# A hybrid decoder layer: prompt heads with the values stationary, two heads in the column halves of TensorE

## The chip, the core and the metric

The kernel runs on one core of one Trainium2 chip, as one launch. The metric is device time in microseconds (us). Three runs of the kernel before gave a median of 1142.3 us (1142.15 to 1143.41). PE is TensorE, ACT ScalarE, DVE VectorE, POOL GpSimd, SP SyncE.

## The reference

One layer for two request groups with the same weights: a prompt of 256 tokens, and 8 sequences that each decode one token after a paged cache of 2048. All is float32.

```
h = x + 1/2 * gate * SwiGLU(norm(x))                        first feed-forward
[q | kv | k_pe | glu | gate_logits] = norm(h) @ w_in
A = latent attention(q, kv, k_pe) @ w_attn_out
B = swish(LayerNorm(DWConv31(GLU(glu)))) @ w_conv_out
h = h + gate_m * ((sigmoid(gA) * A + sigmoid(gB) * B) @ w_out)
y = h + 1/2 * gate * SwiGLU(norm(h))                        second feed-forward
```

What the change touches is the prompt's attention, for 16 heads of 64 value columns, causal over 256 positions:

```
s = einsum('bqhd,bkhd->bhqk', qb, k) * scale
s = where(k_pos <= q_pos, s, -inf)
p = softmax(s, axis=-1)
o = einsum('bhqk,bkhd->bqhd', p, v)
```

## The kernel before

All arrays lie with 128 rows on partitions. Each engine runs one list of instructions, written out by hand, and semaphores tie the lists together (`eng.wait_ge(sem, n)` waits until `sem` has reached `n`, `.then_inc(sem, 1)` counts up at an instruction's end). Nothing reorders the lists: an instruction that waits holds up all that stand behind it on its engine. The layer goes through stages: first feed-forward, projections, **prompt heads**, **128 cache pages** (8 sequences of 16 pages), **gates** (the gate logits' products, with the sums that close both attentions between them), output projections, second feed-forward.

*Prompt heads.* Queries fall in two blocks of 128, so a head has three 128 x 128 blocks of scores: block 0 sees keys 0 to 127, block 1 sees 0 to 255. TensorE makes them in one PSUM bank (`scores`, L2285 and L2286, two banks in turn), VectorE adds the mask and writes all 384 columns to SBUF as `sS`, then takes the maxima of both blocks (`mask_max`, L1581 to L1585), ScalarE takes the exponentials with their row sums `ls` (L1010, L1011), TensorE turns the three blocks (`turn_probs`, L2306, banks 2 and 3), and ScalarE copies them to `pTs` (`turned`, L1003). Then `values` (L2318 to L2321) multiplies: the turned probabilities are the stationary side and 64 columns of `vtok` the moving one, so that queries lie on partitions. After each four heads VectorE multiplies the result with the reciprocals of `ls` into `otok` (`heads_out`, L1593, L1596), token by token. The loop runs scores two heads ahead and values one head behind.

*Around the loop.* `turn_state` (L2295) turns the convolution's state, and ScalarE copies it into `stbuf` (`state_columns`, L996): once in head 15, once after it. `turn` (L2334 to L2341) turns a cached page, ScalarE rounds it to `kTH` (`page_hi`, L1026) and VectorE makes the rest `kTL` (`page_lo`, L1609); `keys` (L1892 to L1894) then multiplies with the weights, three products for each (high and low halves). Page 0's turn stands between the last two heads. GpSimd sets buffers, makes the first convolution rows of the sample group (`sample_rows`, L647 to L655), and later squares the rotary keys of each sequence (L674), which VectorE sums (`rope_squares`, L1651) in page 14 of the sequence.

*Gates.* `turn_heads` (L2424) turns `otok` in four groups of four blocks so that heads lie on partitions, and ScalarE copies them to `oT` (`heads_turned`, L1087), then to `oH` (L1100), the high half for the output projection.

*Page values.* For a sequence's cached values TensorE is used in four column strips of 32 (`page_values`, L2365): four products with 32 stationary columns go to four different groups of 32 partitions of PSUM.

## Time and profile before

| | |
|---|---|
| median of three runs | 1142.3 us |
| the profiled execution | 1141.46 us, of which its span 1139.6 us |
| TensorE | busy 1121.9 us (98%), granted clock 0.997 of full |
| VectorE | busy 779.2 us (68%) |
| ScalarE | busy 581.6 us (51%) |
| GpSimd | busy 68.0 us (6%) |
| chain that ended last | TensorE 94%, VectorE 2% |

The span runs from the first instruction to the last on the core; the time of a run adds what lies around it. The durations of products overlap (a product starts before its predecessor's end), so that what one costs is read from start to start. "PEld" is the loading of the stationary side, which overlaps the products. An instruction on float32 data runs in two passes on TensorE (x2 in the rows), but a turn runs in one.

### The profile page before, as it was taken

What the parts mean: (1) busy time and instruction counts of PE and PEld (TensorE: products, weight loads), DVE (VectorE), ACT (ScalarE), POOL (GpSimd) and SP (SyncE); (2) the same over time, 40 slices, a digit from 0 to 9 for tenths busy, and PEclk for the clock granted to TensorE, in tenths of its full rate; (3) what the DMA queues carried; (4) which work ended last, traced back from release to release, by engine and by line L of the source; (5) the groups of instructions that cost most, each with busy time, mean ns of one, the idle gap of its engine ahead of it and who ended that gap; (6) DMA issues with size and microseconds to landing.
All of it is one profiled execution on the core that took longest, in us unless ns stands there. A gap on an engine that the chain in (4) does not pass through costs nothing.

```text
span 1139.6 us, 25373 instructions
## 1 busy us (share of the span) xinstructions
PE 1121.9 (98%) x9549; PEld 1086.9 (95%) x9549; DVE 779.2 (68%) x1325; ACT 581.6 (51%) x1153; POOL 68.0 (6%) x136
## 2 busy tenths in 40 slices
PE   5999999999999999999999999999999999999998
PEld 3999999999898999999999999999999999999998
DVE  4655553467777688888888888888756666555543
ACT  3444453346576655554545455554567445444432
POOL 2000000010000100101010110101020010000000
PEclk9899999999999999999999999999999999999999
DMA  9997578947344440021211202031257784566562
GB/s 324 316 298 265 184 257 296 349 170 214 100 140 128 130 136 2 22 63 33 52 52 31 64 19 78 11 96 58 67 151 248 231 266 134 181 182 183 172 184 72
DMA packets 165620, 169.77 MB, mean 149 GB/s; under 512 B 25780, under 2 KB 144071, under 8 KB 165525
## 3 DMA queue, kind: packets, MB, share of 16 engines
q1 hardware_dynamic: 163799, 166.83, 46.8%
q10 hardware_dynamic: 1742, 1.88, 0.5%
q8 instruction: 50, 0.82, 0.3%
q14 instruction: 29, 0.24, 0.1%
HBM read 167.13 MB, written 2.49 MB: 149 GB/s over the span
## 4 chain that ended last, share of the span: by engine, by line
PE 94%; DVE 2%; DMA 1%; ACT 1%; SPq 1%; issue 0%; DVEq 0%; ACTq 0%
PE PS L1892 28%; PE PS L1893 27%; PE PS L1894 27%; PE PS L1969 2%; DMA adaw<-in_w_ada 1%; PE PS L2365 1%; PE PS L2340 1%; PE PS L2341 1%; PE PS L2286 1%; PE PS L2097 1%; PE PS L2336 0%; PE PS L2334 0%; PE PS L2285 0%; PE PS L2306 0%; SPq L451 0%
## 5 line engine op out<-in xcount | busy, mean ns | idle before, releaser
L1172 DVE TENSOR_TENSOR wL<-raw,wH 128x1024 fp32r<-128x1024 f32 (+2 forms) x208 | 246.0, 1189 | 210.1 <-ACT wH L717 208.0
L717 ACT ACTIVATE wH<-raw 128x1024 fp32r<-128x1024 f32 (+2 forms) x208 | 213.2, 1029 | 244.6 <-PE PS L1894 221.0
L1892 PE MATMUL PS<-uH,wH 128*128 128x264 f32 x1024 | 294.2, 287 | 3.9 <-DVE uL L1233 3.5
L1893 PE MATMUL PS<-uL,wH 128*128 128x264 f32 x1024 | 291.9, 285 | 0.0
L1894 PE MATMUL PS<-uH,wL 128*128 128x264 f32 x1024 | 291.4, 285 | 0.0
L1892 PE MATMUL PS<-wqH,kTH 128*128 128x336 f32 (+2 forms) x768 | 255.7, 333 | 0.0
L1894 PE MATMUL PS<-wqH,kTL 128*128 128x336 f32 (+2 forms) x768 | 246.0, 320 | 0.0
L1893 PE MATMUL PS<-wqL,kTH 128*128 128x336 f32 (+2 forms) x768 | 245.9, 320 | 0.0
L1892 PEld LDWEIGHTS PS<-uH,wH 128*128 128x128 f32 x1024 | 193.8, 189 | 7.0 <-issue 6.0
L1893 PEld LDWEIGHTS PS<-uL,wH 128*128 128x128 f32 x1024 | 194.2, 190 | 0.0
L1894 PEld LDWEIGHTS PS<-uH,wL 128*128 128x128 f32 x1024 | 193.7, 189 | 0.0
L1614 DVE TENSOR_REDUCE nsum<-sqb 128x16 f32<-128x1024 f32 x128 | 154.9, 1211 | 1.1 <-ACT sqb L1038 1.1
L1893 PEld LDWEIGHTS PS<-wqL,kTH 128*128 128x128 f32 x768 | 144.6, 188 | 0.0
L1892 PEld LDWEIGHTS PS<-wqH,kTH 128*128 128x128 f32 x768 | 144.4, 188 | 0.0
L1894 PEld LDWEIGHTS PS<-wqH,kTL 128*128 128x128 f32 x768 | 144.2, 188 | 0.0
L1038 ACT ACTIVATE sqb<-PS 128x640 f32<-128x640 f32 (+1 forms) x256 | 138.5, 598 | 0.0
L1035 ACT ACTIVATE S<-PS 128x16 f32<-128x16 f32 x128 | 23.3, 182 | 190.9 <-PE PS L1894 190.9
L1701 DVE SCALAR_TENSOR_TENSOR u<-zbuf,wdw,u 128x256 f32<-128x256 f32 x232 | 115.5, 498 | 2.1
L1892 PE MATMUL PS<-aH,wH 128*128 128x264 f32 x352 | 100.6, 286 | 0.0
L1893 PE MATMUL PS<-aL,wH 128*128 128x264 f32 x352 | 100.2, 285 | 0.0
L1894 PE MATMUL PS<-aH,wL 128*128 128x264 f32 x352 | 99.9, 284 | 0.0
L1609 DVE TENSOR_TENSOR kTL<-PS,kTH 128x256 fp32r<-128x256 f32 x128 | 53.9, 421 | 44.2 <-ACT kTH L1026 44.1
(343 smaller groups left out, 1497.4 us busy)
## 6 DMA issues: line engine op xcount, KB each, us to landing
raw<-in_w_ffn_in SPq DMA_DIRECT2D x86, 512.0 KB, 3.6
adaw<-in_w_ada SPq DMA_DIRECT2D x72, 512.0 KB, 6.4
raw<-in_w_ffn_out SPq DMA_DIRECT2D x32, 512.0 KB, 3.6
raw<-in_w_in SPq DMA_DIRECT2D x32, 512.0 KB, 4.4
kv<-in_cache_kv_latent SPq DMA_DIRECT2D x128, 128.0 KB, 2.0
raw<-in_w_ffn_out SPq DMA_DIRECT2D x16, 384.0 KB, 3.1
raw<-in_w_attn_out SPq DMA_DIRECT2D x8, 512.0 KB, 4.4
raw<-in_w_conv_out SPq DMA_DIRECT2D x8, 512.0 KB, 4.1
```

The lines of the kernel that those rows point to most:

```text
L717: f(wH[:, k, 0:width], raw[:, k, 0:width], ACT.Copy).then_inc(w_hi, 1)
L1035: f(S[:, s, n, :], PS[:, b0 + bank, c:c + H], ACT.Copy)
L1038: i_ = f(sqb[:, n % 2, at:at + (k1 - k0) * w].rearrange("p (k w) -> p k w", w=w), PS[:, b0 + k0:b0 + k1, c:c + w], ACT.Square)
L1172: v.tensor_tensor(wL[:, k, 0:width], raw[:, k, 0:width], wH[:, k, 0:width].bitcast(F32), ALU.subtract).then_inc(w_lo, 1)
L1609: v.tensor_tensor(kTL[:, n % 2, :], PS[:, 0, 0:KL], kTH[:, n % 2, :].bitcast(F32), ALU.subtract).then_inc(kTL_done, 1)
L1614: v.tensor_reduce(nsum[:, s, n, :], sqb[:, n % 2, :].rearrange("p (h d) -> p h d", h=H), AX_X, ALU.add).then_inc(knsum_done, 1)
L1701: own.done(v.scalar_tensor_tensor(out=y, in0=z, scalar=w, in1=y, op0=ALU.mult, op1=ALU.add))
L1892: mm(dst, a[0], b[0], start=start, stop=False)
L1893: mm(dst, a[0], b[1], start=False, stop=False)
L1894: return mm(dst, a[1], b[0], start=False, stop=stop)
L1969: i_ = mm(PS[QUAD * g:QUAD * g + NS, bank, 0:P], csil[:, kt, :], w[:, g, :, :], start=(kt == 0), stop=(kt == KT - 1))
L2097: i_ = mm(dst[QUAD * g:QUAD * g + a.shape[1], :], a, parts[g], start=start, stop=stop)
```

## The change

The head loop and its surroundings are written anew; all other stages stay as they are.

- `values(j)` handles two heads. The stationary side is now 64 columns of `vtok` and the moving side the turned probabilities: 256 columns for keys 0 to 127, 128 columns for keys 128 to 255. The first head of the pair writes PSUM partitions 0 to 63, the second 64 to 127. The result already has heads on partitions.
- The result isn't divided at once. VectorE copies it to `oTr`. After the loop it takes all reciprocals in one instruction, TensorE turns them (`turn_sums`) to 16 rows, and VectorE copies these to `rlT`. GpSimd spreads each row over 64 partitions of `rlb` by a transfer within SBUF, eight transfers, then multiplies half of `oTr` (four of eight column blocks), then the same again.
- Scores have three banks, run three heads ahead, and wait for the exponential that empties the bank. The mask is added in place in PSUM, to the two diagonal blocks alone, and the maxima and exponentials read PSUM; `sS` goes. `pTs` has four slots and `nm` too.
- The state is turned and copied in four parts in heads 6, 8, 10 and 12 (of ScalarE's loop), page 0 is turned in head 13 in bank 6, page 1 ahead of the last values.
- GpSimd clears `Pr` before the loop instead of after it. `turn_heads` and `heads_turned` go. ScalarE's `oH` and VectorE's `latent_out` wait for the multiplications (`o_scaled`).

```diff
+STATE_HEADS = (6, 8, 10, 12)
+PAGE_HEAD = 13
...
-        otok = sb("otok", [P, 2, H, VH], at=o)
+        oTr = sb("oTr", [P, KT, SEQ], at=o)
...
-        sS = sb("sS", [P, 2, 384], at=o + 8192)
-        pS = sb("pS", [P, 2, 384], at=o + 11264)
+        pS = sb("pS", [P, 2, 384], at=o + 14592)
         qtokS = qtok[:, 2, 0:H // 4, :]
-        pTs = sb("pTs", [P, 2, 384], at=o + 14336)
+        pTs = sb("pTs", [P, 4, 384], at=o + 8448)
...
+        rlT = sb("rlT", [H, SEQ], at=o + 16640)
...
+        rlb = sb("rlb", [P, 4, SEQ], at=o)
...
+        HEAD_BANK = (0, 7, 1)
+        VALUE_BANK = (4, 5)
+        PAIRS = H // 2
...
-            pool.wait_ge(pv_ps, H)
+            filled(pool, "qt1")
             nc.gpsimd.memset(Pr[:, :, :, :], 0.0)
+            pool.wait_ge(pv_ps, PAIRS)
...
+            def heads_scaled(part):
+
+                for j in range(4):
+                    for m in range(2):
+                        hd = 2 * (4 * part + j) + m
+                        g.dma_start(rlb[VH * m:VH * m + VH, j, :],
+                                    rlT[hd:hd + 1, :].unsqueeze(1).to_broadcast([1, VH, SEQ])).then_inc(in_rl, 16)
+                pool.wait_ge(in_rl, 128 * (part + 1))
+                z = oTr[:, 4 * part:4 * part + 4, :]
+                g.tensor_tensor(z, z, rlb[:, :, :], ALU.mult).then_inc(o_scaled, 1)
+
+            pool.wait_ge(o_sb, 4)
+            pool.wait_ge(rlT_done, 1)
+            heads_scaled(0)
+            pool.wait_ge(o_scaled, 1)
+            heads_scaled(1)
...
             def turned(hd):
                 act.wait_ge(pT_ps, hd + 1)
-                if hd >= 2:
-                    act.wait_ge(pv_ps, hd - 1)
-                f(pTs[:, hd % 2, :], PS[:, 2 + hd % 2, 0:384], ACT.Copy).then_inc(pT_sb, 1)
+                if hd >= 4:
+                    act.wait_ge(pv_ps, (hd - 4) // 2 + 1)
+                f(pTs[:, hd % 4, :], PS[:, 2 + hd % 2, 0:384], ACT.Copy).then_inc(pT_sb, 1)
...
             for hd in range(H):
-                s = hd % 2
+                s, b = hd % 2, HEAD_BANK[hd % 3]
                 act.wait_ge(nmax, hd + 1)
                 if hd >= 2:
                     act.wait_ge(pT_ps, hd - 1)
-                f(pS[:, s, 0:128], sS[:, s, 0:128], ACT.Exp, bias=nm[:, s, 0:1], accum_out=ls[:, 0, hd:hd + 1])
-                f(pS[:, s, 128:384], sS[:, s, 128:384], ACT.Exp, bias=nm[:, s, 1:2], accum_out=ls[:, 1, hd:hd + 1]
-                  ).then_inc(exp_done, 1)
+                f(pS[:, s, 0:128], PS[:, b, 0:128], ACT.Exp, bias=nm[:, hd % 4, 0:1], accum_out=ls[:, 0, hd:hd + 1])
+                f(pS[:, s, 128:384], PS[:, b, 128:384], ACT.Exp, bias=nm[:, hd % 4, 1:2],
+                  accum_out=ls[:, 1, hd:hd + 1]).then_inc(exp_done, 1)
                 if hd >= 1:
                     turned(hd - 1)
-                if hd == 15:
-                    state_columns(0)
+                if hd in STATE_HEADS:
+                    state_columns(STATE_HEADS.index(hd))
+                if hd == PAGE_HEAD + 1:
+                    page_hi(0, 0, 6)
...
-            gate_columns(0)
-            heads_turned(0)
-            heads_turned(1)
-            gate_columns(1)
-            gate_columns(2)
-            heads_turned(2)
-            heads_turned(3)
-            act.wait_ge(ot_sb, 4)
+            for i in range(3):
+                gate_columns(i)
+            act.wait_ge(o_scaled, 2)
...
+            tri = const[:, C_MASK:C_MASK + P].unsqueeze(1).to_broadcast([P, 2, P])
+
             def mask_max(hd):
-                s = hd % 2
+                b = HEAD_BANK[hd % 3]
                 dve.wait_ge(sc_ps, hd + 1)
-                if hd >= 2:
-                    dve.wait_ge(exp_done, hd - 1)
-                v.tensor_tensor(sS[:, s, :], PS[:, s, 0:384], const[:, C_MASK:C_MASK + 384], ALU.add
-                                ).then_inc(masked, 1)
+                if hd >= 4:
+                    dve.wait_ge(exp_done, hd - 3)
+                z = PS[:, b, :].rearrange("p (a n) -> p a n", n=P)[:, 0:3:2, :]
+                v.tensor_tensor(z, z, tri, ALU.add).then_inc(masked, 1)
                 dve.wait_ge(masked, hd + 1)
-                v.tensor_reduce(nm[:, s, 0:1], sS[:, s, 0:128], AX_X, ALU.max, negate=True)
-                v.tensor_reduce(nm[:, s, 1:2], sS[:, s, 128:384], AX_X, ALU.max, negate=True).then_inc(nmax, 1)
+                v.tensor_reduce(nm[:, hd % 4, 0:1], PS[:, b, 0:128], AX_X, ALU.max, negate=True)
+                v.tensor_reduce(nm[:, hd % 4, 1:2], PS[:, b, 128:384], AX_X, ALU.max, negate=True).then_inc(nmax, 1)
 
             def heads_out(g):
 
-                hs = slice(4 * g, 4 * g + 4)
                 if g == 0:
                     dve.wait_ge(written, LAT_WRITTEN)
-                dve.wait_ge(exp_done, 4 * g + 4)
-                own.done(v.reciprocal(rl[:, :, hs], ls[:, :, hs]))
-                own.wait()
-                dve.wait_ge(pv_ps, 4 * g + 4)
-                v.tensor_tensor(otok[:, :, hs, :], PS[:, 4 + g % 2, :].rearrange("p (t h d) -> p t h d", t=2, h=4),
-                                rl[:, :, hs].unsqueeze(3).to_broadcast([P, 2, 4, VH]), ALU.mult).then_inc(o_sb, 1)
-
-            def page_lo(pg, n, b, s, first):
+                dve.wait_ge(pv_ps, 2 * g + 2)
+                v.tensor_copy(oTr[:, 2 * g:2 * g + 2, :].rearrange("p j n -> p (j n)"),
+                              PS[:, VALUE_BANK[g % 2], :]).then_inc(o_sb, 1)
...
-                if hd % 4 == 1 and hd >= 5:
-                    heads_out((hd - 5) // 4)
-            dve.wait_ge(rest_sb, 5)
-            put_q(0, 0)
-            page_lo(0, 0, 0, 0, True)
+                    dve.wait_ge(rest_sb, 5)
+                    put_q(0, 0)
+                if hd % 4 == 2 and hd >= 6:
+                    heads_out(hd // 4 - 1)
+                if hd == PAGE_HEAD + 1:
+                    page_lo(0, 0, 0, 0, True, 6)
+            dve.wait_ge(exp_done, H)
+            v.reciprocal(rl[:, :, :], ls[:, :, :]).then_inc(rl_done, 1)
+            dve.wait_ge(rl_ps, 1)
+            v.tensor_copy(rlT[:, :], PS[0:H, 6, 0:SEQ]).then_inc(rlT_done, 1)
...
+                dve.wait_ge(o_scaled, 2)
...
             def scores(hd):
-                b = hd % 2
+                b = HEAD_BANK[hd % 3]
                 if hd == 0:
                     pe.wait_ge(turned, 4)
-                if hd == 1:
+                if hd == 2:
                     pe.wait_ge(rest_sb, 5)
-                if hd >= 2:
-                    pe.wait_ge(masked, hd - 1)
+                if hd >= 3:
+                    pe.wait_ge(exp_done, hd - 2)
...
-            def values(hd):
-                b, g, hq = 4 + (hd // 4) % 2, hd // 4, hd % 4
-                vc = slice(VH * hd, VH * hd + VH)
-                pe.wait_ge(pT_sb, hd + 1)
-                if hd == 4:
+            def values(j):
+
+                g, q = j // 2, j % 2
+                b = VALUE_BANK[g % 2]
+                pe.wait_ge(pT_sb, 2 * j + 2)
+                if j == 2:
                     pe.wait_ge(mod_turned, ADA_ATTN)
-                if hq == 0 and g >= 2:
+                if q == 0 and g >= 2:
                     pe.wait_ge(o_sb, g - 1)
-                c = slice(VH * hq, VH * hq + VH)
-                mm(PS[:, b, c], pTs[:, hd % 2, 0:128], vtok[:, 0, vc], start=True, stop=True)
-                c = slice(SEQ + VH * hq, SEQ + VH * hq + VH)
-                mm(PS[:, b, c], pTs[:, hd % 2, 128:256], vtok[:, 0, vc], start=True, stop=False)
-                mm(PS[:, b, c], pTs[:, hd % 2, 256:384], vtok[:, 1, vc], start=False, stop=True).then_inc(pv_ps, 1)
+                for m in range(2):
+                    hd = 2 * j + m
+                    mm(PS[VH * m:VH * m + VH, b, SEQ * q:SEQ * q + SEQ], vtok[:, 0, VH * hd:VH * hd + VH],
+                       pTs[:, hd % 4, 0:256], start=True, stop=False)
+                for m in range(2):
+                    hd = 2 * j + m
+                    i_ = mm(PS[VH * m:VH * m + VH, b, SEQ * q + 128:SEQ * q + SEQ], vtok[:, 1, VH * hd:VH * hd + VH],
+                            pTs[:, hd % 4, 256:384], start=False, stop=True)
+                i_.then_inc(pv_ps, 1)
+
+            def turn_sums():
+
+                pe.wait_ge(rl_done, 1)
+                pe.wait_ge(kTL_done, 3)
+                for t in range(2):
+                    i_ = tr(PS[0:H, 6, P * t:P * t + P], rl[:, t, :], ident)
+                i_.then_inc(rl_ps, 1)
...
                     if first and n == 1:
                         pe.wait_ge(o_sb, 4)
-                        pe.wait_ge(st_sb, 4)
+                        pe.wait_ge(rlT_done, 1)
...
-            scores(0)
-            scores(1)
+            for hd in range(3):
+                scores(hd)
             for hd in range(H):
-                if hd + 2 < H:
-                    scores(hd + 2)
                 if hd == 0:
                     mod_rows(ADA_FFN)
                     pe.wait_ge(zst_done, 2)
                 turn_probs(hd)
-                if hd >= 1:
-                    values(hd - 1)
-                if hd == 14:
-                    turn_state(0)
-                if hd == 15:
-                    pe.wait_ge(masked, H)
-                    turn(0, 0, 0, 0, 0, True)
-            values(H - 1)
-            turn_state(1)
-
-
+                if hd + 3 < H:
+                    scores(hd + 3)
+                if hd >= 2 and hd % 2 == 0:
+                    values(hd // 2 - 1)
+                if hd + 1 in STATE_HEADS:
+                    turn_state(STATE_HEADS.index(hd + 1))
+                if hd == PAGE_HEAD:
+                    pe.wait_ge(st_sb, 4)
+                    turn(0, 0, 0, 0, 0, True, 6)
+            turn_sums()
+            turn(0, 0, 1, 1, 0, True)
+            values(PAIRS - 1)
             pe.wait_ge(o_sb, 3)
...
-            def turn_heads(i, bank):
-
-                for kt in range(2 * i, 2 * i + 2):
-                    for t in range(2):
-                        c = SEQ * (kt % 2) + P * t
-                        i_ = tr(PS[:, bank, c:c + P],
-                                otok[:, t, 2 * kt:2 * kt + 2, :].rearrange("p h d -> p (h d)"), ident)
-                i_.then_inc(ot_ps, 1)
...
-            turn_heads(0, 4)
-            turn_heads(1, 5)
...
-            turn_heads(2, 2)
-            turn_heads(3, 3)
```

How the instructions stand:

On TensorE, one head in the middle of the loop before (`pS` holds the probabilities, `pTs` their transposes, `vtok` the values, `PS` is PSUM): scores of the next but one head, three turns, three value products.

```order
L2285 MATMUL PS<-kT,qT 128x128 [waits masked]
L2286 MATMUL PS<-kT,qT 128x256
L2306 MATMUL PS<-const,pS 128x128 [waits pT_sb,exp_done]
L2306 MATMUL PS<-const,pS 128x128 x2
L2318 MATMUL PS<-vtok,pTs 128x64 [waits pT_sb]
L2320 MATMUL PS<-vtok,pTs 128x64
L2321 MATMUL PS<-vtok,pTs 128x64
```

After, two heads of the same stretch:

```order
L2325 MATMUL PS<-const,pS 128x128 [waits pT_sb,exp_done]
L2325 MATMUL PS<-const,pS 128x128 x2
L2303 MATMUL PS<-kT,qT 128x128 [waits exp_done]
L2304 MATMUL PS<-kT,qT 128x256
L2325 MATMUL PS<-const,pS 128x128 [waits pT_sb,exp_done]
L2325 MATMUL PS<-const,pS 128x128 x2
L2303 MATMUL PS<-kT,qT 128x128 [waits exp_done]
L2304 MATMUL PS<-kT,qT 128x256
L2339 MATMUL PS<-pTs,vtok 64x256 [waits pT_sb]
L2339 MATMUL PS<-pTs,vtok 64x256
L2343 MATMUL PS<-pTs,vtok 64x128 x2
```

Scores now wait for an exponential (`exp_done`) and stand behind the turns; the value products come once per two heads, with `vtok` as the stationary side, 64 wide.

On TensorE at the loop's end before (`kr`, `kv` are cached pages, `strow` the convolution state), from page 0's turns, ahead of head 15's values, to the first page product:

```order
L2334 MATMUL PS<-const,kr_110 128x128 [waits kTL_done,kv2_in0,masked]
L2340 MATMUL PS<-const,kv_122 128x128
L2341 MATMUL PS<-const,kv_122 128x128
L2318 MATMUL PS<-vtok,pTs 128x64 [waits pT_sb]
L2320 MATMUL PS<-vtok,pTs 128x64
L2321 MATMUL PS<-vtok,pTs 128x64
L2295 MATMUL PS<-const,strow 128x120 [waits st_sb]
L2295 MATMUL PS<-const,strow 128x120 x7
L2336 MATMUL PS<-qbd,krT 128x64 [waits kTL_done,pT_sb,o_sb]
L2340 MATMUL PS<-const,kv_122 128x128
L2341 MATMUL PS<-const,kv_122 128x128
L1892 MATMUL PS<-wqH,kTH 128x336 [waits qx_done,knsq_done,kTL_done]
```

After, from head 15's turns to the first page product (L1910):

```order
L2325 MATMUL PS<-const,pS 128x128 [waits pT_sb,exp_done]
L2325 MATMUL PS<-const,pS 128x128 x2
L2352 MATMUL PS<-const,rl 16x128 [waits kTL_done,rl_done]
L2352 MATMUL PS<-const,rl 16x128
L2368 MATMUL PS<-qbd,krT 128x64 [waits kTL_done]
L2372 MATMUL PS<-const,kv_122 128x128
L2373 MATMUL PS<-const,kv_122 128x128
L2339 MATMUL PS<-pTs,vtok 64x256 [waits pT_sb]
L2339 MATMUL PS<-pTs,vtok 64x256
L2343 MATMUL PS<-pTs,vtok 64x128 x2
L1910 MATMUL PS<-wqH,kTH 128x336 [waits knsq_done,qx_done,kTL_done,o_sb]
```

The state turns (`strow`) have gone up into the loop, page 0's turns too, and the turns of `rl` (the inverse sums) have come in.

On GpSimd before, from the end of the first convolution rows to the squares of the first sequence (`krq`):

```order
L655 TENSOR_TENSOR u<-u,ztmp 128x8 [waits own_pool]
L674 TENSOR_TENSOR krq<-kr_110 128x512 [waits kTH_done,own_pool]
L676 ISA
L676 ISA gmx<-mx 128x16 [waits mx_done]
L679 COPY snew<-Pr 8x16 [waits p_done]
```

After, the same stretch:

```order
L664 TENSOR_TENSOR ztmp<-ztmp 128x8 [waits own_pool]
L666 TENSOR_TENSOR u<-u,ztmp 128x8 [waits own_pool]
L686 DMA rlb<-rlT 64x1x256 [waits rlT_done,o_sb,own_pool]
L686 DMA rlb<-rlT 64x1x256 x7
L690 TENSOR_TENSOR oTr<-oTr,rlb 128x1024 [waits in_rl]
L686 DMA rlb<-rlT 64x1x256 [waits o_scaled]
L686 DMA rlb<-rlT 64x1x256 x7
L690 TENSOR_TENSOR oTr<-oTr,rlb 128x1024 [waits in_rl]
L702 TENSOR_TENSOR krq<-kr_110 128x512 [waits kTH_done]
L704 ISA
L704 ISA gmx<-mx 128x16 [waits mx_done]
```

Sixteen transfers, `rlb<-rlT`, and two multiplications now stand between the convolution rows and `krq`.

## Rows read from the trace of the kernel before

**Rows 1.** Page, part 1: engine, busy us, share of the span, instructions.
```profile
PE 1121.9 (98%) x9549; PEld 1086.9 (95%) x9549; DVE 779.2 (68%) x1325; ACT 581.6 (51%) x1153; POOL 68.0 (6%) x136
```

**Rows 2.** Windows: stretch, length, then busy us (count) of PE, PEld, DVE, ACT, POOL, PEclk.
```profile
363.02:390.24 27.22, 27.14 (x223) 25.45 (x220) 19.37 (x53) 21.39 (x78) 0.92 (x1) 1.00 0.30 77
...
812.00:860.00 48.00, 48.00 (x462) 46.07 (x461) 31.36 (x49) 30.95 (x48) 9.43 (x10) 1.00 0.46 133
```

**Rows 3.** Timeline, one head: start us, us, engine, line, op, tiles, count, [idle <-releaser].
```profile
360.93 0.40 ACT L1010 ACTIVATE pS<-sS,nm 128x128 f32<-128x128 f32 x1 [0.75 <-DVE nm L1585]
...
367.57 0.56 DVE L1581 TENSOR_TENSOR sS<-PS,const 128x384 f32<-128x384 f32 x1 [0.45 <-PE PS L2286]
...
368.16 0.28 DVE L1584 TENSOR_REDUCE nm<-sS 128x1 f32<-128x128 f32 x1
...
368.32 0.44 PE L2285 MATMUL PS<-kT,qT 96*128 96x128 f32 x2
...
368.37 0.41 DVE L1585 TENSOR_REDUCE nm<-sS 128x1 f32<-128x256 f32 x1
...
368.59 0.60 PE L2286 MATMUL PS<-kT,qT 96*128 96x256 f32 x2
...
368.81 0.40 ACT L1010 ACTIVATE pS<-sS,nm 128x128 f32<-128x128 f32 x1 [0.29 <-DVE nm L1585]
...
369.03 0.49 PE L2306 MATMUL PS<-const,pS 128*128 128x128 f32 x3
...
369.21 0.49 ACT L1011 ACTIVATE pS<-sS,nm 128x256 f32<-128x256 f32 x1
...
369.36 0.33 PE L2318 MATMUL PS<-vtok,pTs 128*128 128x64 f32 x2
...
369.70 0.47 ACT L1003 ACTIVATE pTs<-PS 128x384 f32<-128x384 f32 x1
...
369.97 0.44 PE L2285 MATMUL PS<-kT,qT 96*128 96x128 f32 x2
```

**Rows 4.** Waits of TensorE's weight loads: total us, times, longest.
```profile
PEld PS L2285 <- DVE sS L1581: 0.5, 1, 0.5
```

**Rows 5.** Lines by form, 360 to 390: busy us, mean ns, then idle before.
```profile
L1609 DVE TENSOR_TENSOR kTL<-PS,kTH 128x256 fp32r<-128x256 f32 x1 | 0.4, 424 | 3.1 <-ACT kTH L1026 3.1
...
L1026 ACT ACTIVATE kTH<-PS 128x256 fp32r<-128x256 f32 x1 | 0.4, 378 | 0.0
```

**Rows 6.** Timeline of TensorE around one set of page values (L2365).
```profile
474.44 0.31 PE L1893 MATMUL PS<-wqL,kTH 128*128 128x336 f32 x1
474.58 0.32 PE L1894 MATMUL PS<-wqH,kTL 128*128 128x336 f32 x1
474.83 1.93 PE L2365 MATMUL PS<-kv,Pr 128*32 128x256 f32 x32
476.70 0.33 PE L2334 MATMUL PS<-const,kr 128*128 128x128 f32 x1
```

**Rows 7.** Timeline: the last head's values and the first page product.
```profile
388.38 0.30 PEld L2318 LDWEIGHTS PS<-vtok,pTs 128*128 128x128 f32 x2 [0.32 <-ACT pTs L1003]
...
390.24 0.40 PE L1892 MATMUL PS<-wqH,kTH 128*128 128x336 f32 x1
```

**Rows 8.** Chain of waits, 826 to 828.5: start us, us, what.
```profile
826.82 0.87 PE PS L2424 x8
```

**Rows 9.** Timeline of GpSimd, then VectorE's read of its squares.
```profile
391.24 0.66 POOL L647 TENSOR_TENSOR ztmp<-stbuf,wdw 128x240 f32<-128x240 f32 x1 [0.84 <-ACT stbuf L996]
...
394.27 0.21 POOL L655 TENSOR_TENSOR u<-u,ztmp 128x8 f32<-128x8 f32 x1
429.41 1.04 POOL L674 TENSOR_TENSOR krq<-kr 128x512 f32<-128x512 f32 x1 [34.93 <-ACT kTH L1026]
...
437.49 0.68 DVE L1651 TENSOR_REDUCE ssr<-krq 128x16 f32<-128x512 f32 x1
```

**Rows 10.** SP's page transfers of 128 KB (L425), 362 to 400.
```profile
DMA to landing us min/median/max: 1.9/2.0/5.6
```

83 lines of the change are left out of this document (39 added, 44 removed).

## The prediction

> **What bounds the kernel now.** I read the page first, for which engine fills the span: TensorE is busy 98% of it [rows 1], so a change shortens the kernel only where it takes work from TensorE or removes a moment in which it stands still. The windows view says the same of the two stretches that the change touches: the prompt heads from 363.02, where the first probabilities are turned, to 390.24, where the first page product starts (27.2 us, TensorE busy 27.1), and the gates from 812 (48 of 48) [rows 2]. Then the timeline of one head, to see what TensorE does in it and how far behind it the others are [rows 3]. From start to start: 0.27 for the first score product (L2285), 0.44 for the second (L2286), 0.33 for three turns of the probabilities (L2306), 0.61 for the three value products (L2318 to L2321). That is a period of 1.65 us with no gap. ScalarE works 1.37 of it (0.89 from the first exponential to the copy of the turned probabilities, then 0.47 or 0.48) and waits 0.29. VectorE works 1.25 (0.59, 0.21, then 0.41 and a start) and, once in four heads, 0.9 more for the output.
> The three engines are therefore close together. Taking 0.4 us from TensorE's 1.65 would not give 0.4 per head: ScalarE is next after 0.28.
>
> **The head loop, TensorE's side.** Before, 16 turns of 0.33, 13 pairs of score products of 0.71 (three run before 363.02), 16 times 0.61 for values, 16 state turns and the turns of two pages at about 0.11 each: 5.3 + 9.2 + 9.8 + 1.8 + 0.7 = 26.8 of the 27.2 us; the rest is a wait of 0.3 before the last values [rows 7].
> The change replaces the three value products of a head, whose cost was that of loading 128 stationary columns for 64 moving ones, by products with 64 stationary columns and 256 + 128 moving ones. A 256-column product takes 0.44 [rows 3] and one of 128 half of that, so a head's moving columns cost 0.66. That is no gain if the halves of a pair run one after another (1.31 a pair against 1.22 before, slightly worse), and nearly half if they run beside each other. The trace has the nearest case in four column strips of 32: 16 products of 256 columns in two passes, 32 passes of 0.22, would be 7.0 us in a row and take 1.87 [rows 6]. So strips do run beside each other (1.76 if perfectly). The same rows give the price of going in and out: 0.11 over 1.76 inside, and 0.25 from the last full product's start to the first strip, where its neighbour took 0.14, so 0.21 in all. I take 0.66 + 0.21 = 0.87 a pair; the bounds are 0.66 and 1.31.
> The Trainium skill ("TensorEngine Tiling (Array Packing)", Tiling Modes, Key Properties) says that changing the tiling mode drains TensorE, which speaks against pairs of halves between full-width turns. The trace agrees in kind, with the 0.21 above; by a drain that cost nothing the sum would be 8 x 0.21 = 1.7 us better for TensorE.
> New on TensorE are the two turns of the inverse sums, 0.2 us. The order has three score tiles ahead instead of two, so that the third no longer waits for VectorE's masked copy: 0.5 us, once [rows 4]. With it the turning starts at about 362.5.
>
> **The head loop, the others' side.** ScalarE loses nothing: the exponentials read PSUM instead of SBUF. No row shows an exponential from PSUM; a copy of 256 elements from PSUM takes 378 ns at this place [rows 5], and the exponential of 256 from SBUF 0.49, so I expect no more than 0.05 either way. Inside its loop come four state copies (480 elements, an estimate of 0.5 from the 0.47 for 384; two of the four ran after the loop before) and the two page copies, 0.4 for 256 elements [rows 5] and an estimated 0.3 for 128. VectorE's mask shrinks from 384 elements to 256: 0.42 by the PSUM-reading row of that size [rows 5] against 0.56. Its two reductions now read PSUM, unseen in this trace; bounds are 0 and about 0.1 more each. The reciprocals leave the loop and the output becomes a copy of the same 512 elements. That is 1.25 or less a head, plus 0.17 for the output: it does not bind.
> So TensorE wants (0.33 + 0.71) + 0.87/2 = 1.48 a head, ScalarE 1.37, and I take 1.50. To the end of head 12, TensorE: 362.5 + 13 x 1.04 + 6 x 0.87 + 4 x 0.44 = 383.0. From there ScalarE decides, because no scores are left: its exponential of head 13 ends about 382.6, then copy 0.48, exponential 0.89, copy 0.48, page copies 0.7, exponential 0.89: 386.0. Turning head 15 and copying it: 387.0. The last value pair, with page 1 turned before it under that copy: about 388.0. Before, the page products start at 390.24. Gain in the heads: 2.2 us. Both bounds: with perfect halves ScalarE's own chain from its first exponential at 360.93 [rows 3] is 16 x 1.37 + 2.0 + 0.7 = 24.6, to 385.5, and the last values and starts put the page products at about 386.7, a gain of 3.5; with halves in a row TensorE's sum is 362.5 + 17.2 + 8 x 1.31 = 390.2, plus half a microsecond at the tail: a loss of 0.5.
>
> **The gates.** Sixteen turns of the tokens' outputs go, in two groups of eight at 0.87 [rows 8]: 1.74 us. TensorE has no idle time there [rows 2], and what it does next (the gate products of slots already converted, the sums of the last sequence) is released earlier than it arrives. ScalarE's four copies of turned heads go as well and were hidden. I take the whole 1.7; at worst a wait eats half.
>
> **GpSimd's new work.** It gets 16 transfers of 64 KB inside SBUF and two multiplications of 1024 elements. It worked on its first convolution rows from 391.24, when the last state copy released it, to 394.5, and then stood until 429.41, when it squared the keys' rotary part in 1.04; VectorE reads that at 437.49, by its own order, 7 us after it was ready [rows 9]. Now the state copies are early and the last values release it, at about 388: transfers from 391.4. The multiplications are two of about 2.1 (twice the 512 elements). Transfers issued by GpSimd are in no row: the nearest are SP's of 128 KB, which land 2.0 us after issue [rows 10]. If each took those 2.0 in full and none overlapped, the work would be 391.4 + 32 + 4.2 = 428, still ahead. VectorE waits for it elsewhere only before it writes the first latent row of a sequence pair, two sequences later. While GpSimd multiplies, it may hold VectorE up (no row has the two beside each other on operands as large): between 0 and 2 x 2.1 less a slack of about a microsecond each; I take 0.2.
> The Trainium skill ("SBUF — State Buffer", SBUF: two separate sides, the "DVE blocks DMA" trap) says that a transfer issued by GpSimd is held up while VectorE runs a two-port operation such as a plain fp32 copy or tensor_scalar from SBUF, and gives about 620 ns alone against 3100 ns beside such a copy. Nothing in the trace before can show it, since GpSimd issues no transfer there. It is a rival below.
>
> **Sum.** Against the profiled execution's 1141.46 us (span 1139.6): -2.2 in the heads, -1.7 in the gates, +0.2: 1137.8. The median of the runs lies 0.8 above the profiled one, so 1138.5.
>
> **Rivals.**
> *The halves overlap with no cost and ScalarE alone sets the pace:* 3.5 + 1.7: 1137.1. For it speaks the 1.87 against 7.0; against it the 0.21 at each change of width, and that only two products share the array.
> *The halves run one after another:* the heads lose 0.5, the gates give 1.7: 1141.1. For it: the two passes of one half stand next to each other in the queue, and with two halves instead of four strips a half that is busy holds up the queue sooner. Against it: the strips have that same order. In between, the same time comes if a period is set by the round from scores over mask, maximum and exponential; with three tiles that round has three periods, 4.5 us, for about 3 of work.
> *GpSimd is late (the slower side):* its first squares then hold VectorE at that reduction (437.49, about 435.3 in the new time), the low halves of the next page are late and TensorE stops. The point from which it decides: (435.3 - 1.0 - 391.4 - 4.2 - 4) / 16 = 2.2 us for each transfer. At 3 us each, one and a half times the landing time of [rows 10], it is 16 x 0.8 = 13 us late, and the time would be 1151. By the Trainium skill's 3100 ns it would be 1153, if VectorE ran such copies all the time. But what VectorE runs in this stretch is reductions, two-input operations and PSUM reads, as in [rows 3, 5, 9].
> *The multiplications hold VectorE up:* 2 us more, 1140.5.
>
> **Chances.** Forecast 0.55 (its own range 1137.3 to 1139.7), perfect halves 0.15, halves in a row or a slow round 0.14, VectorE held up 0.08, GpSimd late 0.06, something else 0.02. A change below 0.2% (2.3 us, under 1140.0 or over 1144.6) can't be told from none. Faster: the first two, and a third of the next two, and part of the rest: 0.80. Same 0.12, slower 0.08. The range holds the first three and half of the fourth: 1136.0 to 1141.2.
>
> **What would show it.** A head period of about 1.5 instead of 1.65, with the four value products of a pair inside 0.9; the first page product near 388.0; ScalarE without idle time from head 13 on; no turns of heads between gate products, and TensorE still full there; both multiplications over before 429. Wrong would be a value pair of 1.3 us, a period set by VectorE's mask and reductions, or a gap on TensorE near 435.

## The result and the profile after

The changed kernel takes 1146.5 us (median of 7 runs, 1145.29 to 1147.21) where the kernel before takes 1143.3 on the same chip: a ratio of 1.0033, 95% interval 1.0023 to 1.0042. It is slower: by 3.2 us between the medians, by 3.8 by the ratio. Forecast were 1138.5, and a range of 1136.0 to 1141.2. Its profiled execution took 1145.29, with a span of 1143.4 (before 1139.6).

I laid the two timelines beside each other at points that exist in both, TensorE's own order: the first turn of probabilities, the first page product, the first page values (before L2365, now L2397; they belong to sequence 0 and are made among sequence 1's pages, and the texts written ahead of the runs call them those of sequence 1), and so on. First the end of the heads (timeline of TensorE: start us, us, engine, line, operation, tiles, count); it answers to [rows 7].

```profile
385.92 0.65 PE L2339 MATMUL PS<-pTs,vtok 128*64 128x256 f32 x4
386.40 0.39 PE L2343 MATMUL PS<-pTs,vtok 128*64 128x128 f32 x4
386.72 0.42 PE L1910 MATMUL PS<-wqH,kTH 128*128 128x336 f32 x1
```

The value products of a pair of heads cost 386.72 - 385.92 = 0.80 us, and the first page product starts at 386.72 where it was 390.24: from the first turn of probabilities 24.66 us instead of 27.22. So far the change did more than forecast. 92 us later the lead is gone; the first page values, which [rows 6] has at 474.83, are here:

```profile
478.83 1.93 PE L2397 MATMUL PS<-kv,Pr 128*32 128x256 f32 x32
```

Between the two, 7.5 us were lost. GpSimd's timeline answers to [rows 9]:

```profile
390.65 4.47 POOL L686 DMA_DIRECT2D rlb<-rlT  x8 [0.37 <-POOL u L666]
410.58 2.39 POOL L690 TENSOR_TENSOR oTr<-oTr,rlb 128x1024 f32<-128x1024 f32 x1 [15.46 <-DMA rlb<-rlT]
413.26 2.09 POOL L686 DMA_DIRECT2D rlb<-rlT  x4 [0.29 <-POOL oTr L690]
425.10 0.53 POOL L686 DMA_DIRECT2D rlb<-rlT  x1 [9.74 <-issue]
425.90 1.54 POOL L686 DMA_DIRECT2D rlb<-rlT  x3 [0.27 <-issue]
436.55 2.38 POOL L690 TENSOR_TENSOR oTr<-oTr,rlb 128x1024 f32<-128x1024 f32 x1 [9.11 <-DMA rlb<-rlT]
438.89 1.03 POOL L702 TENSOR_TENSOR krq<-kr 128x512 f32<-128x512 f32 x1
```

Issuing is cheap (8 in 4.47 us), but GpSimd then stands 15.46 us until the eight have landed, and in the second set it even stands 9.74 us in the middle of issuing. Its squares of the rotary keys (krq) come at 438.89 instead of 429.41. The next two views show the rest of the chain, VectorE and then TensorE:

```profile
439.96 0.69 DVE L1668 TENSOR_REDUCE ssr<-krq 128x16 f32<-128x512 f32 x1 [4.49 <-POOL krq L702]
440.68 0.48 DVE L1719 SCALAR_TENSOR_TENSOR u<-zbuf,wdw,u 128x256 f32<-128x256 f32 x1
441.08 0.42 DVE L1621 TENSOR_TENSOR kTL<-PS,kTH 128x256 fp32r<-128x256 f32 x1
```

```profile
437.93 0.34 PE L1912 MATMUL PS<-wqH,kTL 128*128 128x384 f32 x1
441.64 0.68 PE L2368 MATMUL PS<-qbd,krT 128*128 x2 [3.37 <-DVE kTL L1621]
```

The windows of the same stretch (stretch, length, then busy us and count of PE, PEld, DVE, ACT, POOL, then PEclk, DMA share, GB/s) show that the stop costs a second time:

```profile
431.00:436.00 5.00, 5.00 (x34) 4.93 (x34) 3.73 (x6) 2.31 (x7) 0.00 (x0) 1.00 0.74 46
436.00:441.00 5.00, 2.27 (x15) 1.95 (x13) 1.00 (x2) 1.90 (x6) 3.37 (x2) 0.92 0.37 98
441.00:446.00 5.00, 4.36 (x16) 4.37 (x17) 4.77 (x10) 0.39 (x1) 0.00 (x0) 0.50 0.34 89
446.00:451.00 5.00, 5.00 (x32) 4.97 (x31) 1.80 (x3) 3.25 (x8) 0.00 (x0) 0.90 0.75 239
```

During the stop of 3.4 us the granted clock fell to 0.50, its lower level (1.2 of 2.4 GHz), and it stayed there until about 447.0: 16 products in five microseconds instead of 34. That is half of the 4.4 us of work there, and a tenth of the next five: 4.4 x 0.5 + 5 x 0.10 = 2.7 us. An earlier, smaller stop is VectorE's, seen in its timeline beside the first multiplication, with the low half behind it and TensorE's wait:

```profile
410.57 2.67 DVE L1719 SCALAR_TENSOR_TENSOR u<-zbuf,wdw,u 128x256 f32<-128x256 f32 x1
415.70 0.41 DVE L1621 TENSOR_TENSOR kTL<-PS,kTH 128x256 fp32r<-128x256 f32 x1
416.17 0.33 PE L2372 MATMUL PS<-const,kv 128*128 128x128 f32 x1 [1.20 <-ACT sqb L1066]
```

The operation at 410.57 takes 0.48 elsewhere. It began one moment before GpSimd's multiplication and ended 0.3 after it; the low half came at 415.70, and TensorE stood 1.2 us until 416.17. (The profile puts this wait down to ScalarE's squares, which ended at the same moment; what the program waits for at this turn is the low half, `kTL_done`, ready at 416.11.) So the stops and the clock make 3.4 + 2.7 + 1.2 = 7.3 of the 7.5 us. Laid beside the kernel without scaling (e1), instruction by instruction, TensorE falls back by 1.36 at the first stop, 3.57 at the second and 2.56 at the low clock: 7.49.

All profiles of this study go into one table of distances (us, start to start of TensorE instructions). A: first turn of probabilities to first page product. B: from there to the first page values (sequence 0's). C: to those of sequence 6. D: to those of sequence 7, with the first gate products (and the first eight turns) between. E: to the first latent output product (second eight turns). F: from there to the product of the mean.

| kernel | A | B | C | D | E | F |
|---|---|---|---|---|---|---|
| before | 27.22 | 84.59 | 314.02 | 30.02 | 8.75 | 8.65 |
| changed | 24.66 | 92.11 | 314.02 | 29.13 | 7.87 | 10.21 |
| e1 no scaling | 24.64 | 84.62 | 314.02 | 29.12 | 7.88 | 10.21 |
| e2 waits moved | 24.65 | 84.94 | 315.31 | 29.13 | 7.88 | 8.64 |
| e3 SyncE's queue | 24.66 | 112.62 | 314.02 | 29.12 | 7.88 | 10.18 |
| e4 spread source | 24.65 | 86.36 | 314.02 | 29.13 | 7.87 | 10.23 |
| e5 no transfer | 24.65 | 84.62 | 314.02 | 29.12 | 7.88 | 10.21 |
| e6 via device memory | 24.65 | 85.42 | 314.02 | 29.13 | 7.87 | 10.21 |
| e7 idle turns | 24.65 | 84.94 | 315.52 | 30.01 | 8.76 | 8.64 |
| e9 both cures | 24.65 | 84.94 | 315.20 | 29.13 | 7.88 | 10.19 |
| e10 pieces | 24.64 | 84.62 | 314.02 | 29.13 | 7.87 | 10.20 |
| e11 eight turns | 24.65 | 84.62 | 314.02 | 29.12 | 8.76 | 10.20 |
| e12 no narrow products | 24.66 | 84.61 | 314.02 | 29.13 | 7.87 | 6.58 |
| e13 before again | 27.23 | 84.59 | 314.02 | 30.01 | 8.76 | 10.19 |

Where nothing waits, a distance repeats to 0.02 us (F, where it is the longer one, to 0.05), so the steps can be read far more finely than the total, in which the start alone (first scores at 357.9 to 359.9) varies by 2 us. Changed minus before: 0.62 gained in the start, which is such a variation and not the change's, 0.34 from the first scores to the first turning, 2.56 in A, 7.52 lost in B, 0.89 and 0.88 gained in D and E, 1.56 lost in F: 3.8 in all, the difference of the spans.

### The profile page after: what moved, and what is told of

Its sections match the earlier page's. It is cut to its first block, busy times and chain, and to the rows that moved or that the text cites. A ratio compares the mean times of both kernels' runs of the same rounds, so it can differ in the third digit from the quotient of the medians.

```text
span 1143.4 us, 25288 instructions
## 1 busy us (share of the span) xinstructions
PE 1120.4 (98%) x9503; PEld 1080.6 (95%) x9503; DVE 780.2 (68%) x1323; ACT 578.0 (51%) x1149; POOL 79.9 (7%) x154
## 3 DMA queue, kind: packets, MB, share of 16 engines
q0 software_dynamic: 512, 1.05, 2.5%
## 4 chain that ended last, share of the span: by engine, by line
PE 88%; DMA 3%; DVE 2%; SPq 2%; ACT 1%; POOL 1%; issue 1%; DVEq 0%; ACTq 0%; POOLq 0%
PE PS L1910 26%; PE PS L1911 26%; PE PS L1912 26%; DMA rlb<-rlT 2%; PE PS L1987 2%; SPq L461 2%; PE PS L2397 1%; PE PS L2372 1%; PE PS L2373 1%; DMA raw<-in_w_ffn_in 1%; POOL rlb L686 1%; PE PS L2304 1%; PE PS L2115 1%; PE PS L2325 1%; PE PS L2368 0%
## 5 line engine op out<-in xcount | busy, mean ns | idle before, releaser
L1910 PE MATMUL PS<-uH,wH 128*128 128x264 f32 x1024 | 294.1, 287 | 4.3 <-DVE uL L1247 3.7
L1910 PE MATMUL PS<-wqH,kTH 128*128 128x336 f32 (+2 forms) x768 | 256.7, 334 | 0.0
L1910 PEld LDWEIGHTS PS<-uH,wH 128*128 128x128 f32 x1024 | 193.9, 189 | 7.9 <-issue 6.2
L1910 PEld LDWEIGHTS PS<-wqH,kTH 128*128 128x128 f32 x768 | 145.2, 189 | 0.2 <-issue 0.2
L1063 ACT ACTIVATE S<-PS 128x16 f32<-128x16 f32 x128 | 23.3, 182 | 196.0 <-PE PS L1912 196.0
L1719 DVE SCALAR_TENSOR_TENSOR u<-zbuf,wdw,u 128x256 f32<-128x256 f32 x232 | 117.8, 508 | 2.1
L1910 PE MATMUL PS<-aH,wH 128*128 128x264 f32 x352 | 100.6, 286 | 0.0
```

Source lines behind the costliest of these rows:

```text
L1063: f(S[:, s, n, :], PS[:, b0 + bank, c:c + H], ACT.Copy)
L1719: own.done(v.scalar_tensor_tensor(out=y, in0=z, scalar=w, in1=y, op0=ALU.mult, op1=ALU.add))
L1910: mm(dst, a[0], b[0], start=start, stop=False)
```

## The experiments

Each is the changed kernel with the edit shown. Ratios are to the kernel before, run beside it: its median was 1142.3 us with e1 to e4, 1143.4 with e5 to e9, and 1142.0 with e10 to e13, so compare experiments of different groups by their ratios or by the table.

**e1: no transfers, no multiplications.**
```
-            heads_scaled(0)
-            pool.wait_ge(o_scaled, 1)
-            heads_scaled(1)
+            pool.sem_inc(o_scaled, 2)
```


> The changed kernel without the 16 transfers of the inverse sums and without GpSimd's two multiplications (the heads stay unscaled, so its output is another). Theory (all of the loss lies in the late transfers and in what TensorE waits for behind them): TensorE does not stop at 415 and 441, the page values of sequence 1 start near 471.4 where the changed kernel has 478.9, and the time is 1146.5 - 7.5 = about 1139.0. Rival A (the gates' clock drop near 833 follows from the missing turns alone): the granted clock of 0.50 stays there and costs its 1.6 us, and the time is the same 1139.0. Rival B (the drop follows from the earlier stop): it goes, and the time is 1137.4. Rival C (the heads in column halves or the gates cost more than the transfers): above 1143.

Measured: 1137.95 us, ratio to before 0.9964 (0.9951 to 0.9976). B is 84.62, the distance of the kernel before. The whole loss in B comes from the scaling. F still has its 1.56, so this drop is not a consequence of the stop at 441 (against Rival B). That it follows from the missing turns, the rest of Rival A, is not shown by this; e13 speaks against it.

**e2: the waits moved.**
`heads_scaled` is cut into `spread`, its eight transfers, and `scaled`, its wait and multiplication.
```
-            heads_scaled(0)
-            pool.wait_ge(o_scaled, 1)
-            heads_scaled(1)
+            spread(0)
...
                 nc.gpsimd.tensor_tensor(krq[:, :, :], kr, kr, ALU.mult).then_inc(kr_sq, 1)
+                if b == 0:
+                    scaled(0)
+                    pool.wait_ge(o_scaled, 1)
+                    spread(1)
...
                     sample_rows(b + 1)
+                if b == 0:
+                    scaled(1)
```


> All work of the changed kernel, in another order on GpSimd: the first eight transfers are issued where they are now, but krq of sequence 0 goes ahead of their wait and of the first multiplication, the second eight are issued behind that, and their multiplication stands behind the sampled rows of sequence 1. Theory (lateness of GpSimd is what cost): landings take as long as before, nobody waits for them, krq comes near 427 and VectorE's ssr does not wait; 1139 to 1140.5, the 1 us above the kernel without scaling being what the two multiplications hold VectorE up. Rival (the transfers hurt by filling the DMA engines, so that page loads or VectorE suffer too): stays at 1143 or more.

Measured: 1138.88 us, ratio 0.9974 (0.9964 to 0.9984): faster than before with all of the changed kernel's work in it. GpSimd's timeline:

```profile
390.59 4.47 POOL L686 DMA_DIRECT2D rlb<-rlT  x8 [0.37 <-POOL u L666]
425.81 1.04 POOL L703 TENSOR_TENSOR krq<-kr 128x512 f32<-128x512 f32 x1 [30.75 <-ACT kTH L1045]
426.81 2.40 POOL L693 TENSOR_TENSOR oTr<-oTr,rlb 128x1024 f32<-128x1024 f32 x1
429.50 2.11 POOL L686 DMA_DIRECT2D rlb<-rlT  x4 [0.29 <-POOL oTr L693]
441.47 2.08 POOL L686 DMA_DIRECT2D rlb<-rlT  x4 [9.86 <-issue]
```

The transfers are as slow as before (the issuing still stands 9.86 us) and nobody waits for them. What is left, 0.32 in B and 1.3 in C, comes within 9 us after each multiplication's end (TensorE waits 0.59 and 0.22 for low halves after the second).

**e3: the same 16 transfers from SyncE's queue.** `spread` with `sp.dma_start`; GpSimd keeps its waits and multiplications:
```
+            sp.wait_ge(o_sb, 4)
+            sp.wait_ge(rlT_done, 1)
+            spread(0)
             sp.wait_ge(ada_used, ADA_ATTN)
             gate_quad(0)
             first_pages(1, range(4))
+            sp.wait_ge(o_scaled, 1)
+            spread(1)
```

> The same 16 transfers at the same places in the order of data, issued by SyncE's queue (the hardware queue of the page loads) instead of by GpSimd; GpSimd only waits and multiplies. Theory S (software-made transfers are slow in themselves): eight land within 5 us, first multiplication near 396, second near 402, krq in time, 1139 to 1140.5. Theory P (each transfer reads 64 times the same row of one partition, and that is slow from any queue): eight still take 15 to 20 us, the loads behind them on SyncE's queue come later, and the time is 1146 or more.

Measured: 1166.01 us (ratio 1.0209, 1.0192 to 1.0226). The queue's timeline, and then waits of ScalarE and TensorE (total us, times, longest):

```profile
392.35 12.62 SPq L447 DMA_DIRECT2D rlb<-rlT  x8
405.07 6.25 SPq L407 DMA_DIRECT2D raw<-in_w_in  x4
```

```profile
ACT wH L753 <- DMA raw<-in_w_in: 23.2, 6, 14.5
PE PS L2380 <- DVE kTL L1629: 12.8, 1, 12.8
PE PS L2376 <- DVE kTL L1629: 9.9, 1, 9.9
```

Theory P: the eight landed at 411.9, no sooner than from GpSimd's queue. And here the weights behind them on the queue come late (ScalarE waits up to 14.5 us for them), which stopped VectorE's splits and TensorE for 12.8 us. The wait of 9.9 is the old one: krq comes at 460.25. That GpSimd issued the transfers was not the harm; it kept them off the loads' queue.

**e4: the same size and queue, each row read from another partition.**
```
-    rlT[hd:hd + 1, :].unsqueeze(1).to_broadcast([1, VH, SEQ])
+    oTr[VH * m:VH * m + VH, 4 * part + j, :]
```


> The changed kernel with 16 transfers of the same size on the same queue of GpSimd, but each of the 64 rows of 1 KB is read from a partition of its own (the attention heads' rows themselves) instead of 64 times from one; the factors are not the inverse sums, so the output is another. Theory P (one partition's row read by all engines is the limit): eight land in 3 to 5 us and the multiplications come near 397 and 405. Theory S (software-made transfers are slow whatever they read): eight land in 15 to 20 us as in the changed kernel, multiplications near 410 and 436.

Measured: 1140.44 us in one run, multiplications at 402.0 and 413.6 (I had put them at 397 and 405; the first set took 10.4 us instead of 3 to 5, 4.5 of it issuing, beside loads that kept the DMA engines fully busy from 396 to 404). From the DMA view of 385 to 440 (queue, packets, MB, share of 16 engines; then KB each and median us to landing), the changed kernel and e4:

```profile
q0 software_dynamic: 512, 1.05, 51.1%
...
raw<-in_w_in SPq DMA_DIRECT2D x4, 512.0 KB, 15.2
rlb<-rlT POOLq DMA_DIRECT2D x16, 64.0 KB, 9.2
```

```profile
q0 software_dynamic: 512, 1.05, 6.8%
...
raw<-in_w_in SPq DMA_DIRECT2D x4, 512.0 KB, 8.8
rlb<-oTr POOLq DMA_DIRECT2D x16, 64.0 KB, 2.6
```

The same bytes in the same packets occupy the DMA engines 7.5 times as long when each transfer reads one partition's row 64 times. It is the source, neither the queue nor the size. Loads of weights beside them land later too (15.2 against 8.8 us); nobody waited for those here. From the first issue to the multiplication, the first eight transfers (0.52 MB) took 19.9 us, 26 GB/s; from SyncE's queue it was 19.6, 27 GB/s; the second eight, with the stop in their issuing, took 23.3.
The Trainium skill ("SBUF — State Buffer", Door 1: The DMA port swizzle) says that DMA bandwidth depends on how many of 16 ports the partitions of a transfer reach, and gives about 27 GB/s for one port. By that the 0.52 MB would take 19 us, an estimate from the page's figure; the trace agrees with its 19.9 and 19.6. Whether one port, one partition or the re-reading of the same bytes in SBUF is the limit was not tried apart.

**e5: multiplications without transfers.**
```
-                g.tensor_tensor(z, z, rlb[:, :, :], ALU.mult).then_inc(o_scaled, 1)
+                g.tensor_tensor(z, z, z, ALU.mult).then_inc(o_scaled, 1)
```

> The changed kernel without the 16 transfers; GpSimd still runs its two multiplications (each row group by itself, so the output is another), back to back from about 391. It prices what the multiplications alone cost through VectorE. Theory: two operations of 2.4 us, each holding one of VectorE's operations to about 2.7 us and TensorE for up to 1.2 us behind it: the kernel without any scaling (1137.95 measured) plus 0.5 to 2.4, about 1139.2. Rival (the holding is absorbed, it only showed because transfers ran beside it): 1138.0, no stop of TensorE between 390 and 420.

Measured: 1138.07 us, ratio 0.9961 (0.9947 to 0.9976), B 84.62, no stop: the rival. Run from 390.2 to 394.2, the multiplications cost TensorE nothing: VectorE is idle for 2.5 us until 391.3 and has little to do, and what they add to its operations (0.3 us at 391.6, 0.5 at 393.5) is absorbed. (They took 1.96 each here, reading one tile.) My theory took a stop that depends on its place for a fixed cost.

**e6: sums through device memory.**
```
+            g.dma_start(x["scr"], rlT[:, :]).then_inc(in_rl, 16)
+            pool.wait_ge(in_rl, 16)
...
-                        g.dma_start(rlb[VH * m:VH * m + VH, j, :],
-                                    rlT[hd:hd + 1, :].unsqueeze(1).to_broadcast([1, VH, SEQ])).then_inc(in_rl, 16)
+                rows = x["scr"].rearrange("(k m) n -> m k n", m=2)
+                for m in range(2):
+                    g.dma_start(rlb[VH * m:VH * m + VH, :, :],
+                        rows[m, 4 * part:4 * part + 4, :].unsqueeze(0).to_broadcast([VH, 4, SEQ])).then_inc(in_rl, 16)
```


> The changed kernel in its own order on GpSimd, but the inverse sums are written once to device memory (16 KB) and spread from there: two transfers of 256 KB for each half, issued by GpSimd as before. Theory P (what made the 16 transfers slow is the 64-fold reading of one partition's row): the write 2 us, each half 3 to 5 us, multiplications near 398 and 406, krq in time, 1139 to 1140.5 as with the rows read from 64 partitions. Rival (256 KB written into 64 partitions by GpSimd's queue is slow whatever is read, or reads of one row in device memory are as slow): halves land 15 us or more after their issue, 1144 to 1147.

Measured: 1138.93 us, ratio 0.9965 (0.9954 to 0.9977). Its transfers, in the same view:

```profile
q0 software_dynamic: 352, 1.07, 7.0%
...
rlb<-scr_rl POOLq DMA_DIRECT2D x4, 256.0 KB, 5.9
scr_rl<-rlT POOLq DMA_DIRECT2D x1, 16.0 KB, 2.2
```

Theory P again, with a right output and GpSimd's order unchanged: multiplications at 402.5 and 414.0 (I had put them at 398 and 406), krq in time, no stop but one of 0.6. B is 0.8 above the floor.

**e7: the gates' turns put back into e2,** on a constant.
```
             pe.wait_ge(knsq_done, PAGES + 2)
+            idle_turns(4)
+            idle_turns(5)
             gate_pair(1)
...
             gate_pair(2)
+            pe.wait_ge(g_free, G_GATE + 3)
+            idle_turns(2)
+            idle_turns(3)
```

> The kernel with the waits moved (1138.88 measured), with 16 turns of a constant put back on TensorE in the gates at the two places where the kernel before turned the heads (nobody reads them). Prices the gates' part alone. Theory (16 turns are 1.74 us of an unbroken TensorE): 1140.6. Rival (turns hid something or the clock falls less with them in place): no difference, 1138.9.

Measured: 1140.80 us (ratio 0.9988, 0.9979 to 0.9998) against 1138.88 (0.9974), and D and E grow by 0.88 each. The gates' step is worth 1.76 us, all of it on the path.

**e9: the edits of e2 and e6 together** (the diffs above).

> Both cures: waits moved behind krq and behind the sampled rows of sequence 1, and the sums spread through device memory. Theory (in the kernel with the waits moved nobody waits for a transfer any more): 1138.9, the same as that kernel within 0.1%. Rival (the 16 slow transfers still cost through page loads or VectorE): 1138.0, as without any scaling.

Measured: 1140.61 us, ratio 0.9979 (0.9967 to 0.9990), 0.15% above e2 in the median and 0.05% in the ratio to before; the intervals overlap. Its distances are e2's within 0.11, except for F (10.19 against 8.64), and its profiled execution starts its scores 1.9 us later. On B and C the theory holds: slow transfers that nobody waits for cost nothing.

**e10: e6 with each multiplication in four pieces of 128x256.**
```
-                z = oTr[:, 4 * part:4 * part + 4, :]
-                g.tensor_tensor(z, z, rlb[:, :, :], ALU.mult).then_inc(o_scaled, 1)
+                for k in range(4):
+                    z = oTr[:, 4 * part + k, :]
+                    i_ = g.tensor_tensor(z, z, rlb[:, k, :], ALU.mult)
+                i_.then_inc(o_scaled, 1)
```


> The kernel with the sums spread through device memory, in the changed kernel's order, with each multiplication of 128x1024 in four pieces of 128x256. Theory (GpSimd's multiplication holds one operation of VectorE until it ends, so the hold is as long as the piece): pieces of 0.6 us each, VectorE's longest operation beside them about 1.1 us, and from the first page product to the page values of sequence 1 it takes 84.6 to 84.9 us where it took 85.4 with whole multiplications; 1138.2 to 1138.6. Rival (the hold is the sum of the work, whatever its pieces): 85.4 again, 1138.9.

Measured: 1137.48 us, ratio 0.9955 (0.9942 to 0.9969), 0.7 below the range expected, and B 84.62, the floor, as expected. GpSimd, then VectorE beside its first pieces:

```profile
404.18 3.02 POOL L690 TENSOR_TENSOR oTr<-oTr,rlb 128x256 f32<-128x256 f32 x4 [8.15 <-DMA rlb<-scr_rl]
```

```profile
405.10 0.80 DVE L1722 SCALAR_TENSOR_TENSOR u<-zbuf,wdw,u 128x256 f32<-128x256 f32 x1
405.82 1.21 DVE L1629 TENSOR_REDUCE nsum<-sqb 128x16 f32<-128x1024 f32 x1
406.95 1.05 DVE L1722 SCALAR_TENSOR_TENSOR u<-zbuf,wdw,u 128x256 f32<-128x256 f32 x2
```

VectorE's operation with two inputs is held to 0.8 us, not 2.67, and its reduction beside a piece not at all. The work on GpSimd grew (four pieces 3.0 against 2.4) and the harm went. The pieces also came 1.3 and 1.5 us later after the first page product than e6's multiplications did, and e5 shows that the place matters: that single operations are held for less is shown, how much of the 0.80 us in B is due to that and how much to the place is not. The Trainium skill ("SBUF — State Buffer", SBUF: two separate sides) has the rule: a GpSimd operation that reads SBUF and a VectorE operation with two SBUF inputs exclude each other for a whole instruction. The trace agrees, with 2.67 and 0.80 us for the operation with two inputs and 1.21 for the reduction, which has one.
This is the kernel to keep: it is faster than the kernel before and than the changed one.

**e11: e10 with eight idle turns ahead of the latent output's products.**
```
+            pe.wait_ge(g_free, G_GATE + 3)
+            for bank in (2, 3):
+                for t in range(4):
+                    tr(PS[:, bank, P * t:P * t + P], ident, ident)
             pe.wait_ge(ol_done, NB // 2 + 1)
```

> The same with 8 turns of a constant put on TensorE directly ahead of the narrow products of the latent output in the gates (where the kernel before turned its second eight). Theory (those turns, 0.87 us, keep the granted clock up there, which saves 1.57 us where it falls): no stretch at 0.50 near 830, 0.7 us less than the kernel in pieces. Rival (the clock falls or not by something else): it falls as in most of the kernels without turns, and the time is 0.9 us more.

Measured: 1139.31 us, ratio 0.9973 (0.9961 to 0.9985); E grows by 0.89 and F keeps its 10.20. The rival, in this profile: the turns did not hold the clock up. Over the table, F is the longer one in 2 of the 4 profiles with turns at this place (e11, e13; not in the first of before, nor in e7) and in 8 of the 9 without (not in e2), so that the turns make the fall rarer is not excluded.

**e12: e10 without the eight narrow products of the latent output.**
```
-                for pr in range(NB // 2):
-                    c = 128 * kt + QUAD * pr
-                    i_ = mm(PS[:, 0, c:c + QUAD], olrow[:, pr, 128 * kt:128 * kt + 128],
-                            sel, start=False, stop=(pr == NB // 2 - 1))
```

> The kernel in pieces without the 8 narrow products of 32 columns of the latent output in the gates (only the two products of 8 rows stay, so the outputs of the samples are others). Theory (the narrow products ahead of it are what the clock falls for): the granted clock stays 1.00 from 800 to 850. Rival: it falls to 0.50 near 830 all the same.

**e13: the kernel before, profiled again,** without an edit.

> The kernel before once more, for a second profile. Theory (with the turns of the heads in the gates the clock holds): granted clock 1.00 from 800 to 850, and 8.65 us from the first latent output product to the mean's product, as in the first profile. Rival (the drop is a matter of the execution, not of the kernel): a stretch at 0.50 there in this one, 10.2 us.

Measured: 1135.36 and 1143.99 us, one run each. Windows over the same products of the kernel before in this second profile (e13), of e10 and of e12 (columns as above):

```profile
827.00:830.00 3.00, 3.00 (x25) 2.67 (x24) 1.30 (x2) 2.26 (x4) 0.00 (x0) 1.00 0.77 220
830.00:833.00 3.00, 3.00 (x21) 2.88 (x22) 1.53 (x5) 2.83 (x9) 0.00 (x0) 0.84 0.72 197
833.00:836.00 3.00, 3.00 (x17) 3.00 (x17) 1.82 (x6) 0.03 (x1) 0.00 (x0) 0.59 0.11 37
```

```profile
824.00:827.00 3.00, 3.00 (x25) 2.84 (x25) 2.00 (x3) 3.00 (x10) 0.00 (x0) 0.96 0.70 184
827.00:830.00 3.00, 3.00 (x15) 3.00 (x15) 2.51 (x8) 0.31 (x2) 0.00 (x0) 0.50 0.58 168
```

```profile
824.00:827.00 3.00, 3.00 (x26) 2.88 (x25) 2.17 (x4) 3.00 (x8) 0.00 (x0) 1.00 0.73 201
827.00:830.00 3.00, 3.00 (x27) 3.00 (x26) 3.00 (x8) 1.70 (x4) 0.00 (x0) 1.00 0.69 178
```

PEclk, the third number from the end, falls in the kernel before too (F 10.19), so the 1.56 us of F, which looked like a price of the change in the first pair of profiles, also comes without the change and differs between executions of one kernel. Without the narrow products, one profile shows no drop; but 3 of the 13 profiles with them show none either, so that they bring it about is a guess.

## Why the prediction was wrong

- **The step that failed** is "If each took those 2.0 in full and none overlapped, the work would be 391.4 + 32 + 4.2 = 428, still ahead". From the first issue (390.65) to the end of the second multiplication (438.93) GpSimd took 48.3 us, not 36 (436.55 + 2.38 is the end). Without the multiplications that is 2.7 us for each transfer of half the size, above the 2.2 from which the rival "GpSimd is late" decides. I took the landing time of [rows 10], page loads whose rows come from device memory into many partitions, as a price that can only be too high for half the bytes. But a transfer's price depends on what it reads; the changed access (one row 64 times) was in the diff. e4 and e6 show it: with other sources the second multiplication began at 413.6 and 414.0, 22 us and more ahead of the changed kernel's.
- **The rival** "GpSimd is late" came about by its mechanism and place: squares, VectorE's reduction, low halves, TensorE. Its chance of 0.06 was too small for a threshold only a tenth above a price I had not seen. The trap that the prediction takes from the Trainium skill ("SBUF — State Buffer", SBUF: two separate sides), transfers held up behind VectorE, was not the reason: from SyncE's queue (e3) the same transfers are as slow, and with another source (e4) GpSimd's are fast.
- **The price of a stop** is more than its length. I had none of the clock in it; 3.4 us of standing cost about 2.6 more.
- **VectorE held by the multiplications**: forecast 0.2; 0.00 (e5) to 1.74 (e4) by where they fall, 1.36 in the changed kernel (1.2 of it as a wait). The bounds held; the value was a mean over places that I could not know.
- **The heads**: forecast 2.2, with 0.5 of it from the third score tile. Measured 0.34 ahead of the turning and 2.56 in A: 2.9. The mechanism was right. The pair cost 0.80, not 0.87 (0.6 us over eight): going in and out of the halves costs 0.14 over the 0.66 of moving columns, not 0.21. The period is 1.46 (two heads from 365.97 to 368.89), not 1.50; the rival "perfect halves" had said 3.5.
- **The gates**: forecast 1.74, measured 1.77 (table) and by addition 1.76 (e7). Right.
- Without the late transfers the time comes near the forecast: e6, e1 and e10 ran at 1138.9, 1138.0 and 1137.5 where 1138.5 was forecast. In part that is luck: in e1 the stretches that the change touches give 0.3 + 2.6 + 1.8 = 4.7 us where 3.9 was forecast for them, and how often F is the longer one, before and after, was in no term.
